# The third unit of the first attention's values goes between the pooling's products and the near products, and every later unit of both attentions goes one level sooner

## The chip, the cores and the metric

The kernel runs on one core of a Trainium2 chip. The metric is the device time of one execution in microseconds (us), lower is better.

## What is computed

A chain of blocks over a sequence of 512 tokens of width 1024, batch 1, all in float32: two hybrid layers (banded attention and chunkwise retention side by side), a SwiGLU feed-forward, a token mixer, a second feed-forward and a last norm. The change lies in the token mixer. Its input is projected by one weight matrix and split over four mixers, each 256 channels wide:

```python
p = (u @ w_in).astype(jnp.float32)
p_pool, p_hg, p_rw, p_gla = jnp.split(p, [G, 5 * G, 5 * G + RWKV_COLS], axis=-1)
y_pool = causal_multiscale_pool(p_pool, pool_w, pool_b, pool_scale)
hq, hf, hi, hg = jnp.split(p_hg, 4, axis=-1)
o_h = chunked_gated_linear_attention(silu(hq) * QK_SCALE, 1.0 - f, hi, log_f)      # HGRN
y_hgrn = rms_norm_2(o_h, hgrn_norm) * jax.nn.sigmoid(hg)
...                                                                              # RWKV-7 from p_rw
gq, gk, gv, gg, ga = jnp.split(p_gla, [G, 2 * G, 3 * G, 4 * G], axis=-1)
log_a = jax.nn.log_sigmoid(ga @ gla_w2 + gla_b) / GLA_GATE_TAU
o_g = chunked_gated_linear_attention(gq * QK_SCALE, gk, gv, log_a)                 # GLA
...
y = jnp.concatenate([y_pool, y_hgrn, y_rwkv, y_gla], axis=-1) @ w_out
```

Both linear attentions, the first ("hgrn") and the second ("gla"), have the form S_t = diag(a_t) S_(t-1) + k_t v_t, o_t = q_t S_t, with 4 heads of 64 channels.

## The kernel before, in words

**Engines and order.** The program is written out by hand, one instruction list for each engine, and semaphores tie them. Nothing reorders it: each engine works through its list, and waits at an instruction until the named semaphores have come.

**Units.** All large weights are streamed as units of 128x1024 (512 KB). SyncE loads a unit into one of four `raw` slots, in the order of a table (`unit_order`, L165 to L167). ScalarE (ACT) makes its rounded high part `w_high`, VectorE (DVE) the rest `w_low` (`split_through`, one instruction each on L2033 and L1260; these two lines are helpers, and most activations and tensor operations of the kernel have them), TensorE (PE) multiplies in three passes (`three_passes`, L500, L501, L502), 24 matmuls of 512 columns. There are three `w_high` and `w_low` slots. `use()`, called on ACT and DVE once for each unit in the places where PE takes it, makes the split of the unit two behind. PE waits for "weights split" of its unit.

**A linear attention.** `linear_attention(name, fill)` exists on PE, ACT and DVE. It first calls `fill(0)`. Then PE waits for the running sums of the decays ("decay summed") and makes the near products (L852, 32 matmuls of 128 columns in two pairs of banks), which DVE masks (`sb_near`). Then come nine levels, n from 0 to 8. On PE:

```python
for n in range(len(ORDER)):
    if n + 1 < len(ORDER):
        fill(n + 1)
    ...
    scores(n)
if name == "gla":
    fill(len(ORDER))
values()
if name == "hgrn":
    fill(len(ORDER))
```

`scores(n)` waits for "factors" of its level: DVE takes differences of the decays (`sb_E<-sb_c_hgrn`), ACT their exponential (`sb_E<-sb_E`), DVE multiplies with keys and queries (`sb_E<-sb_E,sb_kq_hgrn`). The products of levels 0 to 5 are on L865, those of the next ones on L876 and L879, `values()` on L891. `fill` is what is put between the levels: other work of the mixers, above all units.

**What the fills hold.** In the first attention: 4 units of its own values (tiles `w_mix_tok`, group 0), then `others`, 5 units for the second attention (gate, two queries, two keys; between the gate's unit and the first query's the small gate products `sb_ga,sb_gla_w` on L482), then 2 of the 4 units of the second attention's values. In the second one: the other 2, and 8 units for RWKV (`rwkv_steps`), with key norms (L482, from the squares `sb_y_rwkv` that ACT makes of mixed keys) and gates between them. DVE lands each RWKV unit (`sb_shifted<-bank,sb_inv_rms`) and mixes it.

**Values.** A value group holds four PSUM banks from its first unit to its last. When the last is done, ACT lands the four banks (`sb_v_hgrn`, `sb_v_gla`, "v landed by S"), and only then may their next users have them.

**Beside them.** At the head of the first attention stand the pooling's products (`pool_outputs`, L482 `sb_window,sb_pool_w`), whose four banks ACT reads (`sb_y_pool`). The end of the first attention's norm, `finish_hgrn` (square, sum and reciprocal on DVE, root on ACT `sb_small`), stands in the second one's `fill(0)`.

Of the kernel before, what the change touches and what calls it, by code (L numbers as in the profile page):

```python
# [141 lines left out]
def unit_order(t):  # L142

    order = []
    for n in range(2):
        product = lambda g: [t["w_tok"][n, g, u] for u in range(4)]
        order += [t["w_rot"][n, f] for f in range(8)] + product(0) + product(1) + product(2)
        order += [t["w_qk"][n, f] for f in QK_ORDER] + [t["w_ag"][n, f] for f in range(4)]
        order += [t["w_out"][n, g, half, pair] for g, half, pair in OUT_STEPS]

    def feed_forward(which):
        units = [t["w_ffn_in"][which, f] for f in range(2 * FT)]
        return units + [t["w_ffn_out"][which, f][:, a:min(a + UNIT, D_FF)]
                        for f in range(KT) for a in range(0, D_FF, UNIT)]

    def mixer_tiles(*tiles):
        return [t["w_mix_f"][f] for f in tiles]

    def mixer_group(g):
        return [t["w_mix_tok"][g, u] for u in range(4)]  # L160

    order += feed_forward(0)
    order += mixer_tiles(0, 1)
    order += mixer_tiles(10, 12, 11, 13) + mixer_group(0)
    order += [t["w_mix_ga"]] + mixer_tiles(14, 16, 15, 17)  # L165
    values, projections = mixer_group(1), mixer_tiles(*range(2, 10))
    order += values[0:3] + [projections[0], values[3]] + projections[1:]  # L167
    order += [t["w_mix_out"][f] for f in range(KT)] + [t["w_mix_out_rwkv"][u] for u in range(2)]
    return order + feed_forward(1)

# [282 lines left out]
def tensor_engine(e, s, mem, units):  # L453
# [371 lines left out]
    def mixers():  # L825
        m, n = mem.mix, MIX_NORM
# [123 lines left out]
        values_h, others, values_g = token_major("v", "hgrn", 1, n), gla_steps(), token_major("v", "gla", 1, n)  # L950

        def fill_hgrn(n):
            if n == 0:
                next(values_h)
                next(values_h)
                pool_outputs()
            else:
                next(values_h if n < 3 else others if n < 8 else values_g)

        linear_attention("hgrn", fill_hgrn)  # L960
        turn_values("hgrn", 0)
# [36 lines left out]
        projections = rwkv_steps()  # L998

        def fill_gla(n):  # L1000
            if n < 2:
                next(values_g)
                next(projections)
            elif n < 6:
                next(projections)
                if n == 4:
                    key_norms()
                if n in (2, 4):
                    next(projections)
                if n == 5:  # L1010
                    p.mark("xg read", MIX_NORM)
            elif n == 6:
                low_rank_gates()
            elif n == 9:
                output_gate()
# [233 lines left out]
def vector_engine(e, s, mem, units):  # L1249
# [359 lines left out]
    def mixers():  # L1609
# [157 lines left out]

        def fill_hgrn(n):
            if n == 0:
                next(values_h)  # L1770
                next(values_h)
            else:
                next(values_h if n < 3 else others if n < 8 else values_g)

        finish_hgrn = linear_attention("hgrn", fill_hgrn, lambda n: None, lambda n: None)

# [54 lines left out]

        def fill_gla(n):
            if n < 6:
                if n < 2:
                    next(values_g)
                if n == 0:
                    finish_hgrn()
                next(projections)
                if n in (2, 4):
                    next(projections)  # L1840
                    if n == 4:
                        floor_norms()
                    next(projections)
            elif n == 8:
                operand_steps()
# [175 lines left out]
def scalar_engine(e, s, mem, units, t):  # L2021
# [273 lines left out]
    def mixers():  # L2295
# [121 lines left out]
        def fill_hgrn(n):  # L2417
            if n == 0:
                next(values_h)
                next(values_h)  # L2420
                a.wait_ge(*of("pool shift"))
                for f in range(2):
                    for r in (slice(0, 64), slice(64, 128)):
                        a.wait_ge(*of("pool out", f, r.start))
                        act(m.y_pool[r, f, :], bank("pool out", f, r.start)[r, :], "y pool", f, r.start,
                            scale=mem.col("pool_scale", f, r), bias=small[r, 168 + f:169 + f])
            else:
                next(values_h if n < 3 else others if n < 8 else values_g)

        finish_hgrn = linear_attention("hgrn", fill_hgrn)  # L2430
        land_mixed("hgrn")
# [45 lines left out]
        projections = rwkv_steps()  # L2477

        def fill_gla(n):
            if n < 2:  # L2480
                next(values_g)
                if n == 0:
                    finish_hgrn()
                next(projections)
            elif n < 6:
                if n == 5:
                    low_rank_tanh()
                    spread_norms()
                next(projections)
                if n == 3:  # L2490
                    square_keys()
                if n in (2, 4):
                    next(projections)
            elif n == 6:
                sigmoids()
            elif n == 7:
                raise_decays()
            elif n == 9:
                land_gate()
# [431 lines left out]
```

## Time and profile before

| what | us |
|---|---|
| three runs | 1681.21, 1682.84, 1686.25 |
| their median | 1682.84 |
| the profiled execution, its own time | 1683.53 |
| its span | 1681.4 |
| PE busy in the span | 1638.9 (97%) |
| DVE busy | 862.1 (51%) |
| ACT busy | 667.8 (40%) |
| mean granted clock of TensorE | 0.986 |

The own time is the device time of the same execution that the trace shows; 2.1 us of it lie outside the span. Busy time is by the trace's instruction records. The first attention stands at about 988 to 1073 us of the span, the second at 1074 to 1161.

### The profile page before, as it was taken

How to read it: one execution, taken by the hardware profiler on the slowest of the kernel's cores; microseconds unless marked ns; L12 is line 12 of the kernel's file. 1: busy time of each engine (PE TensorE's matmuls, PEld its weight loads, DVE VectorE, ACT ScalarE, POOL GpSimd, SP SyncE). 2: the span in 40 equal slices, each digit the busy share in tenths (PEclk: the TensorE clock that was granted, in tenths of full speed). 3: DMA queues.
4: the chain of work that ended last, by engine and by line, in shares of the span. 5: the costliest groups of instructions: out<-in, count | busy, mean ns of one | idle time of the engine just before them, and what ended most of it. 6: DMA issues, size and time to landing. Idle time of an engine off the chain costs nothing.

```text
span 1681.4 us, 23771 instructions
## 1 busy us (share of the span) xinstructions
PE 1638.9 (97%) x9520; PEld 1328.4 (79%) x9520; DVE 862.1 (51%) x1170; ACT 667.8 (40%) x1018; POOL 127.2 (8%) x127
## 2 busy tenths in 40 slices
PE   9999999999999999999999999997999999999997
PEld 6877778877777888888888878785877888888886
DVE  6733445552444565444433478668557554444333
ACT  6145565314656433333323355346433433333221
POOL 0001001000100110000000310000410200000000
PEclk9999999999999999999999999998899999999998
DMA  5412212341221323322333322220012233222331
GB/s 181 154 63 76 88 51 88 113 126 63 71 81 51 101 76 112 100 91 98 91 96 102 135 81 65 63 63 1 14 36 82 88 101 100 94 94 84 102 103 50
DMA packets 40749, 144.13 MB, mean 86 GB/s; under 512 B 4816, under 2 KB 4832, under 8 KB 40256
## 3 DMA queue, kind: packets, MB, share of 16 engines
q1 hardware_dynamic: 37296, 131.61, 24.6%
q0 software_dynamic: 2192, 8.87, 1.6%
q10 hardware_dynamic: 1152, 2.14, 0.4%
q8 instruction: 75, 1.23, 0.3%
q14 instruction: 34, 0.28, 0.1%
HBM read 140.50 MB, written 2.10 MB: 85 GB/s over the span
## 4 chain that ended last, share of the span: by engine, by line
PE 88%; DVE 7%; ACT 3%; issue 1%; DMA 0%; DVEq 0%; SPq 0%; ACTq 0%
PE bank L500 26%; PE bank L502 25%; PE bank L501 25%; PE bank L482 2%; PE bank L1044 2%; PE bank L488 2%; PE bank L865 1%; PE bank L667 1%; PE bank L731 1%; PE bank L710 1%; DVE sb_w_low L1260 1%; ACT sb_w_high L2033 1%; PE bank L589 0%; DMA sb_x<-xT 0%; DVE sb_near L1674 0%
## 5 line engine op out<-in xcount | busy, mean ns | idle before, releaser
L1260 DVE TENSOR_TENSOR sb_w_low<-sb_raw,sb_w_high 128x1024 fp32r<-128x1024 f32 (+1 forms) x253 | 312.1, 1234 | 365.5 <-ACT sb_w_high L2033 359.0
L500 PE MATMUL bank<-sb_xg_high,sb_w_high 128*128 128x512 f32 x1176 | 465.4, 396 | 1.4 <-DVE sb_w_low L1260 1.4
L502 PE MATMUL bank<-sb_xg_high,sb_w_low 128*128 128x512 f32 x1176 | 458.7, 390 | 0.0
L501 PE MATMUL bank<-sb_xg_low,sb_w_high 128*128 128x512 f32 x1176 | 458.6, 390 | 0.0
L2033 ACT ACTIVATE sb_w_high<-sb_raw 128x1024 fp32r<-128x1024 f32 (+1 forms) x253 | 263.2, 1040 | 347.4 <-PE bank L502 323.2
L500 PEld LDWEIGHTS bank<-sb_xg_high,sb_w_high 128*128 128x128 f32 x1176 | 221.1, 188 | 63.3 <-issue 15.8
L502 PEld LDWEIGHTS bank<-sb_xg_high,sb_w_low 128*128 128x128 f32 x1176 | 221.2, 188 | 46.8
L501 PEld LDWEIGHTS bank<-sb_xg_low,sb_w_high 128*128 128x128 f32 x1176 | 221.3, 188 | 44.6 <-issue 0.2
L502 PE MATMUL bank<-sb_h_high,sb_w_low 128*128 128x512 f32 x352 | 136.9, 389 | 0.0
L500 PE MATMUL bank<-sb_h_high,sb_w_high 128*128 128x512 f32 x352 | 136.9, 389 | 0.0
L501 PE MATMUL bank<-sb_h_low,sb_w_high 128*128 128x512 f32 x352 | 136.9, 389 | 0.0
L500 PE MATMUL bank<-sb_w_high,sb_xg_high 128*128 128x512 f32 x256 | 103.0, 402 | 0.0
L501 PE MATMUL bank<-sb_w_low,sb_xg_high 128*128 128x512 f32 x256 | 100.1, 391 | 0.0
L502 PE MATMUL bank<-sb_w_high,sb_xg_low 128*128 128x512 f32 x256 | 99.9, 390 | 0.0
L2647 POOL TENSOR_TENSOR sb_square_sum<-sb_square_sum,sb_square 128x512 f32<-128x512 f32 x20 | 26.1, 1306 | 748.5 <-ACT sb_square L2033 748.5
L500 PEld LDWEIGHTS bank<-sb_h_high,sb_w_high 128*128 128x128 f32 x352 | 66.1, 188 | 13.8
L501 PEld LDWEIGHTS bank<-sb_h_low,sb_w_high 128*128 128x128 f32 x352 | 66.1, 188 | 13.7
L502 PEld LDWEIGHTS bank<-sb_h_high,sb_w_low 128*128 128x128 f32 x352 | 66.1, 188 | 13.6
L2033 ACT ACTIVATE sb_h_high<-sb_up 128x512 fp32r<-128x512 f32 x44 | 27.8, 632 | 115.6 <-DVE sb_up L1260 115.6
L1260 DVE TENSOR_TENSOR sb_up<-bank,sb_inv_rms 128x512 f32<-128x512 f32 x44 | 30.4, 691 | 78.0 <-PE bank L502 77.1
L2033 ACT ACTIVATE sb_gate<-sb_gate 128x512 f32<-128x512 f32 x44 | 27.8, 632 | 92.3 <-DVE sb_gate L1260 92.3
L500 PEld LDWEIGHTS bank<-sb_w_high,sb_xg_high 128*128 128x128 f32 x256 | 48.3, 189 | 17.1 <-issue 7.1
(344 smaller groups left out, 1965.9 us busy)
## 6 DMA issues: line engine op xcount, KB each, us to landing
sb_raw<-w_ffn_in SPq DMA_DIRECT2D x88, 512.0 KB, 3.5
sb_raw<-w_ffn_out SPq DMA_DIRECT2D x32, 512.0 KB, 3.5
sb_raw<-w_tok SPq DMA_DIRECT2D x24, 512.0 KB, 3.6
sb_raw<-w_mix_f SPq DMA_DIRECT2D x18, 512.0 KB, 3.5
sb_raw<-w_rot SPq DMA_DIRECT2D x16, 512.0 KB, 3.6
sb_raw<-w_qk SPq DMA_DIRECT2D x16, 512.0 KB, 3.4
sb_raw<-w_out SPq DMA_DIRECT2D x16, 512.0 KB, 3.4
sb_raw<-w_ffn_out SPq DMA_DIRECT2D x16, 384.0 KB, 3.1
```

The costliest lines, as they stand in the source:

```text
L482: made = e.matmul(out, lhsT, rhs, start=n == 0, stop=n == len(pairs) - 1)
L488: made = e.transpose(banks[i][:, blk(n)], in_, mem.ident)
L500: e.matmul(out, w[0], v[0], start=first, stop=False)
L501: e.matmul(out, w[0], v[1], start=False, stop=False)
L502: return e.matmul(out, w[1], v[0], start=False, stop=last)
L667: made = e.matmul(out[k], m.feat["rk"][r, f, blk(j)], m.feat["rq"][r, f, j * P:], start=part == 0, stop=part == 1)
L710: e.matmul(out[k], m.qT[r, j, blk(q)], m.kT[r, j, 0:keys], start=True, stop=True).then_inc(*p.up("scores", n, 2 * j + k, q))
L731: made = e.matmul(out[64 * k:64 * k + 64, blk(q)], m.tok["av"][:, key, h * ATT_DIM:(h + 1) * ATT_DIM], m.probT[:, 2 * (q % 2) + k, blk(key ...
L1044: made = e.matmul(out(banks[i], t, c), left(t, c), right(t, c), start=True, stop=True)
L1260: e.tensor_tensor(out, a, b, op).then_inc(*v.up(*signal))
L2033: e.activation(out, in_, func, bias=bias, scale=scale, accum_out=accum).then_inc(*a.up(*signal))
L2647: e.tensor_tensor(out, a, b, op).then_inc(*g.up(*signal))
```

## The change

The kernel text changes in the table of units and in the fills of the three engines.

- `fill_hgrn(0)` takes three value units instead of two. On PE the third stands behind `pool_outputs`, ahead of the near products. On ACT it stands behind the landing of the pooling's outputs.
- `fill_hgrn(n)`: the fourth value unit at n = 1 (before: the third at 1, the fourth at 2), the five `others` at n = 2 to 6 (before 3 to 7), three units of the second attention's values at n = 7, 8, 9 (before two, at 8 and 9).
- `fill_gla(0)` takes the last value unit of the second attention and the first of RWKV, `fill_gla(1)` only the second of RWKV.
- The table: the four value units of the second attention come together, then RWKV's. SyncE so loads the fourth ahead of RWKV's first.

No instruction is added or taken away.

```diff
@@ unit_order @@
-    values, projections = mixer_group(1), mixer_tiles(*range(2, 10))
-    order += values[0:3] + [projections[0], values[3]] + projections[1:]
+    order += mixer_group(1) + mixer_tiles(*range(2, 10))
@@ TensorE, fill_hgrn @@
                 next(values_h)
                 next(values_h)
                 pool_outputs()
+                next(values_h)
             else:
-                next(values_h if n < 3 else others if n < 8 else values_g)
+                next(values_h if n < 2 else others if n < 7 else values_g)
@@ TensorE, fill_gla @@
-            if n < 2:
+            if n == 0:
                 next(values_g)
-                next(projections)
-            elif n < 6:
+            if n < 6:
                 next(projections)
@@ VectorE, fill_hgrn @@
             if n == 0:
-                next(values_h)
-                next(values_h)
+                for _ in range(3):
+                    next(values_h)
             else:
-                next(values_h if n < 3 else others if n < 8 else values_g)
+                next(values_h if n < 2 else others if n < 7 else values_g)
@@ VectorE, fill_gla @@
             if n < 6:
-                if n < 2:
+                if n == 0:
                     next(values_g)
-                if n == 0:
                     finish_hgrn()
                 next(projections)
@@ ScalarE, fill_hgrn @@
                         act(m.y_pool[r, f, :], bank("pool out", f, r.start)[r, :], "y pool", f, r.start,
                             scale=mem.col("pool_scale", f, r), bias=small[r, 168 + f:169 + f])
+                next(values_h)
             else:
-                next(values_h if n < 3 else others if n < 8 else values_g)
+                next(values_h if n < 2 else others if n < 7 else values_g)
@@ ScalarE, fill_gla @@
-            if n < 2:
+            if n == 0:
                 next(values_g)
-                if n == 0:
-                    finish_hgrn()
-                next(projections)
-            elif n < 6:
+                finish_hgrn()
+            if n < 6:
                 if n == 5:
```

In the order of instructions, this is TensorE between the pooling's products and the near products, before and then changed (bank numbers are PSUM banks; in brackets the semaphores that a row waits for):

```order
L482 MATMUL bank4<-sb_window_1_145,sb_pool_w_1_124 64x512 [waits pooled,hgrn_q_landed]
L482 MATMUL bank5<-sb_window_1_145,sb_pool_w_1_124 64x512 [waits hgrn_k_landed]
L852 MATMUL bank2<-sb_kq_hgrn_1_130 128x128 [waits y_pool,decay_summed]
L852 MATMUL bank3<-sb_kq_hgrn_1_130 128x128
```
```order
L481 MATMUL bank5<-sb_window_1_145,sb_pool_w_1_124 64x512 [waits hgrn_k_landed]
L499 MATMUL bank6<-sb_w_high_1_51,sb_xg_high_1_66 128x512 [waits weights_split]
L500 MATMUL bank6<-sb_w_low_1_52,sb_xg_high_1_66 128x512
L501 MATMUL bank6<-sb_w_high_1_51,sb_xg_low_1_67 128x512
L852 MATMUL bank2<-sb_kq_hgrn_1_130 128x128 [waits y_pool,decay_summed]
```

The third value unit (bank 6, 24 rows of which three stand here) now waits for its split ahead of the near products; its place behind them is taken by the fourth. VectorE at the same place, before and then changed (`sb_c_hgrn` the decays, `sb_E` the factors):

```order
L1280 SCALAR_TENSOR_TENSOR sb_c_hgrn_131<-sb_mixer_120,sb_c_hgrn_131 128x512 x2
L1260 TENSOR_TENSOR sb_E_136<-sb_c_hgrn_131 128x16x32 x2
L1260 TENSOR_TENSOR sb_w_low_52<-sb_raw_50,sb_w_high_51 128x1024 x2
L1260 TENSOR_TENSOR sb_E_136<-sb_E_136,sb_kq_hgrn_130 128x1024
L1260 TENSOR_TENSOR sb_near_138<-bank,sb_shared_54 128x512 x4
L1260 TENSOR_TENSOR sb_E_137<-sb_c_hgrn_131 128x32x16 x2
```
```order
L1279 SCALAR_TENSOR_TENSOR sb_c_hgrn_131<-sb_mixer_120,sb_c_hgrn_131 128x512 x2
L1259 TENSOR_TENSOR sb_E_136<-sb_c_hgrn_131 128x16x32 x2
L1259 TENSOR_TENSOR sb_w_low_52<-sb_raw_50,sb_w_high_51 128x1024 x3
L1259 TENSOR_TENSOR sb_E_136<-sb_E_136,sb_kq_hgrn_130 128x1024
L1259 TENSOR_TENSOR sb_near_138<-bank,sb_shared_54 128x512 x4
L1259 TENSOR_TENSOR sb_E_137<-sb_c_hgrn_131 128x32x16 x2
```

A third split joins the two; the first of them is the third value unit's in both. ScalarE from the end of the first attention into the second (`sb_small` the root of the norm), before and then changed:

```order
L2033 ACTIVATE sb_w_high_51<-sb_raw_50 128x1024
L2033 ACT_TABLE_LOAD
L2033 ACTIVATE sb_small_60<-sb_small_60 128x4
L2033 ACTIVATE sb_w_high_51<-sb_raw_50 128x1024
L2033 ACTIVATE sb_mixed_147<-sb_shifted_148,sb_small_60 128x512
L2033 ACT_TABLE_LOAD
L2033 ACTIVATE sb_E_137<-sb_E_137 128x1024
L2033 ACTIVATE sb_w_high_51<-sb_raw_50 128x1024
L2033 ACTIVATE sb_v_gla_135<-bank,sb_inv_rms_t_59 128x512 x4
```
```order
L2031 ACTIVATE sb_w_high_51<-sb_raw_50 128x1024
L2031 ACTIVATE sb_v_gla_135<-bank,sb_inv_rms_t_59 128x512 x4
L2031 ACT_TABLE_LOAD
L2031 ACTIVATE sb_small_60<-sb_small_60 128x4
L2031 ACTIVATE sb_w_high_51<-sb_raw_50 128x1024
L2031 ACTIVATE sb_mixed_147<-sb_shifted_148,sb_small_60 128x512
L2031 ACT_TABLE_LOAD
L2031 ACTIVATE sb_E_137<-sb_E_137 128x1024
```

The landing of the second attention's values moved from behind the first mixing of RWKV to a place ahead of the norm's root.

## Rows read from the trace of the kernel before

**Rows 1.** Page, busy time of each engine.
```profile
PE 1638.9 (97%) x9520; PEld 1328.4 (79%) x9520; DVE 862.1 (51%) x1170; ACT 667.8 (40%) x1018; POOL 127.2 (8%) x127
```
**Rows 2.** Waits of PE: releaser, us in total, times, longest us.
```profile
PE bank L876 <- DVE sb_E L1260: 7.2, 1, 7.2
```
**Rows 3.** Timeline, PE, head of first attention: start, us, operation, [idle before <-releaser].
```profile
988.81 1.93 PE L482 MATMUL bank<-sb_window,sb_pool_w 64*64 64x512 f32 x8
...
992.37 1.16 PE L852 MATMUL bank<-sb_kq_hgrn 64*128 64x128 f32 x16 [1.63 <-ACT sb_y_pool L2033]
...
994.10 1.99 PE L852 MATMUL bank<-sb_kq_hgrn 64*128 64x128 f32 x16 [0.57 <-ACT sb_y_pool L2033]
...
996.01 0.79 PE L500 MATMUL bank<-sb_w_high,sb_xg_high 128*128 128x512 f32 x1
...
1004.38 0.50 PE L500 MATMUL bank<-sb_w_high,sb_xg_high 128*128 128x512 f32 x1
...
1010.05 2.00 PE L865 MATMUL bank<-sb_E 64*128 64x64 f32 x32
```
**Rows 4.** Timeline, DVE and ACT at the same place.
```profile
991.99 1.42 DVE L1260 TENSOR_TENSOR sb_E<-sb_c_hgrn 128x512 f32<-128x512 f32 x2
993.51 2.55 DVE L1260 TENSOR_TENSOR sb_w_low<-sb_raw,sb_w_high 128x1024 fp32r<-128x1024 f32 x2
994.03 1.28 ACT L2033 ACT_TABLE_LOAD   x1
...
995.33 1.06 ACT L2033 ACTIVATE sb_E<-sb_E 128x1024 f32<-128x1024 f32 x1
...
997.74 3.08 DVE L1260 TENSOR_TENSOR sb_near<-bank,sb_shared 128x512 f32<-128x512 f32 x4
...
1008.69 1.06 ACT L2033 ACTIVATE sb_w_high<-sb_raw 128x1024 fp32r<-128x1024 f32 x1
...
1010.16 2.85 ACT L2033 ACTIVATE sb_v_hgrn<-bank,sb_inv_rms_t 128x512 f32<-128x512 f32 x4 [0.41 <-PE bank L502]
```
**Rows 5.** Windows: stretch, us, PE, PEld, DVE, ACT, POOL busy, PEclk, DMA share, GB/s.
```profile
994.24:997.65 3.41, 3.41 (x20) 2.89 (x21) 2.95 (x3) 2.13 (x2) 0.00 (x0) 0.50 0.52 156
...
1021.54:1024.96 3.42, 3.42 (x9) 2.77 (x9) 3.07 (x5) 0.78 (x2) 0.00 (x0) 0.50 0.00 0
```
**Rows 6.** Timeline, PE, gate products and first query unit of the second attention.
```profile
1019.58 1.98 PE L482 MATMUL bank<-sb_ga,sb_gla_w 16*128 16x512 f32 x4
...
1021.49 0.78 PE L500 MATMUL bank<-sb_xg_high,sb_w_high 128*128 128x512 f32 x1
```
**Rows 7.** Timeline, head of the second attention: PE, ACT, DVE.
```profile
1074.40 0.48 PE L500 MATMUL bank<-sb_w_high,sb_xg_high 128*128 128x512 f32 x1
...
1078.31 1.28 ACT L2033 ACT_TABLE_LOAD   x1
...
1079.93 0.39 PE L500 MATMUL bank<-sb_xg_high,sb_w_high 128*128 128x512 f32 x1
...
1082.14 0.21 ACT L2033 ACTIVATE sb_small<-sb_small 128x4 f32<-128x4 f32 x1 [2.55 <-DVE sb_small L1276]
...
1082.38 0.18 DVE L1272 RECIPROCAL sb_small<-sb_small 128x4 f32<-128x4 f32 x1 [0.27 <-ACT sb_small L2033]
```
**Rows 8.** Timeline, DVE, ACT and PE on the way to the second attention's long wait.
```profile
1100.43 1.23 DVE L1260 TENSOR_TENSOR sb_w_low<-sb_raw,sb_w_high 128x1024 fp32r<-128x1024 f32 x1 [2.72 <-ACT sb_w_high L2033]
...
1123.73 1.48 ACT L2033 ACTIVATE sb_y_rwkv<-sb_mixed,sb_cols 128x512 f32<-128x512 f32 x2
...
1127.69 1.84 PE L482 MATMUL bank<-sb_mixer,sb_y_rwkv 128*128 128x2 f32 x16
...
1135.17 0.69 DVE L1260 TENSOR_TENSOR sb_shifted<-bank,sb_inv_rms 128x512 f32<-128x512 f32 x1 [2.35 <-PE bank L502]
...
1142.77 0.69 DVE L1260 TENSOR_TENSOR sb_shifted<-bank,sb_inv_rms 128x512 f32<-128x512 f32 x1 [0.70 <-PE bank L502]
...
1159.52 2.08 PE L876 MATMUL bank<-sb_E 64*128 64x128 f32 x16 [7.19 <-DVE sb_E L1260]
```

## The prediction

> **What bounds the kernel now.** I read four views in this order: the page, the waits of PE, the timeline of the two linear attentions on PE, DVE and ACT, and the windows of granted clock. The page says that PE is busy for 97% of the span [rows 1], so a reordering that leaves every instruction in place can only win PE's idle time and its slow stretches, or add to them. The view of PE's waits names one long one, 7.2 us for a factor of the second attention [rows 2]; the timeline puts its end at 1159.52 [rows 8]. The place that the change aims at is small: after the pooling's products, which end at 990.74, PE waits 1.63 us, then 0.57 us, for ACT's reads of the pooling's banks [rows 3]. Behind this idle time the clock is granted at 0.50 (1.2 GHz) from 994.24 to 997.65, against 1.00 (2.4 GHz) elsewhere [rows 5]; matmuls run there at half speed, so it costs half of 3.41, 1.7 us. All these sums are made against the profiled execution's 1683.53 us, 0.7 us above the median of the three runs, 1682.84. About 0.3%, 5 us, is what a measurement of this kernel can tell from no change.
>
> **1. The head of the first attention.** The third value unit is now ahead of the near products, and waits for its split. DVE makes that split as the first of two from 993.51 to 996.06 [rows 4], behind the running sums and the differences at 991.99, which stand ahead of it in both orders. Nothing upstream is earlier than before, so the split is ready at 993.51 + 1.28 = 994.8. PE is idle from 990.74 to 994.8, 4.06 us, in place of 1.63 + 0.57. Then it does the unit: 5.53 us by the neighbouring units of rows 7 (1074.40 to 1079.93), and if the slow stretch ends where it did, 2.85 us of it lie at half speed, which adds 1.43: about 1001.7. Near products: 32 in two pairs, each pair about 1.16 us as the first does [rows 3], to 1002.9 and 1004.0. The fourth unit: to 1009.6. Meanwhile DVE, which masks the near products in four steps (3.08 us), starts them at 1002.9 instead of 997.74, and comes to 1006.0, then the next differences (1.42) to 1007.5; ACT follows with an exponential and a split, 1.06 each [rows 4], to 1009.7, and only then lands the values, four steps in 2.85. The first level's products on PE used two banks that the near products had left; in the new order they take two of the values' banks, and wait for two landings, 1.43 us: 1011.2. They take 2.0 us as the next level's do [rows 3]: 1013.2. Before, the same work (four value units, near products, first level) was done at 1010.05 [rows 3]. **Cost: +3.2 us.** The bounds: if the landing comes right behind the fourth unit and the near products are hidden as before, 1009.6 + 1.4 + 2.0 gives 1013.0; if the low clock lasts as long after 994.8 as it did before after 994.24, 0.3 us more. The third split that DVE now makes in the pair costs 1.23 us of DVE at a place where it afterwards waits for PE (near products at 1002.9), so nothing; the table load and first exponential on ACT slip by one split, 1.06, under the same cover. SyncE's loads: two units of 512 KB change places, both still up to four slots ahead of their use; nothing, and if that cover were gone, ACT's split would wait for `sb_raw`.
>
> **2. One unit more ahead of the second attention.** Twelve units instead of eleven stand there, 5.6 us [rows 7]. **+5.6** on everything from its head: RWKV's first unit starts at 1079.93 + 3.2 + 5.6 = 1088.7. PE gets this unit back inside the second attention, but that stretch ends on something else (4).
>
> **3. The root of the first attention's norm.** ACT's list now has the landing of the second attention's values, 2.85 us [rows 4], ahead of the table load (1.28) and the root (0.21) [rows 7]. The landing waits for the last value unit, 1088.7; so 1088.9 + 2.85 + 1.28 + 0.21, and the gaps between them give the reciprocal on DVE at about 1093.35, against 1082.38 [rows 7]: +10.95, of which 8.8 are steps 1 and 2. **+2.15.** Queued behind the reciprocal on DVE are two products, a weight split and the landing of RWKV's first unit; behind the root on ACT a split and the first mixing. All of it is late with it.
> The Trainium skill ("ScalarE: Activation LUTs", What ACT_TABLE_LOAD costs) has a drain of about 1.38 us beside a load of about 1.28. The row shows the load at 1.28, and the next activation starts 0.02 us behind it [rows 4]. By the page the table load that now stands in the path would cost 1.4 us more (an estimate from that page), by the row nothing; I go by the row.
>
> **4. The second attention.** From the reciprocal (1082.38) to the last factors, released at 1159.5 [rows 8], DVE is nearly without a pause; this chain of 77 us, and not PE, sets when the attention ends, since PE waits 7.19 us for it. The change takes out of it: one split, 1.23 us and its gap, 1.33; the wait of 2.72 us for ACT's split, which stood behind the values' landing [rows 8] (landed earlier now); the wait of 2.35 us for RWKV's seventh unit, since PE now has a unit less in front; and of the wait of 0.70 for the eighth a part. How much of it hangs on the key norms: ACT's key squares end at 1125.2 and PE's norms start at 1127.69 [rows 8], 2.5 us later. The squares follow DVE, late by 10.95 - 1.33 - 2.72 = 6.9, so they end at 1132.1; PE would be there at 1127.69 + 3.2 = 1130.9 or sooner, waits, and is late by 4.4 from there. DVE, late by 6.9 - 2.35 = 4.55, is then released by PE again at 4.45: 0.1 of the 0.70. **-6.5.** Bounds: -7.1 (all of 0.70) and -5.8 (the 0.70 and 0.6 of the 2.35 stay, if PE is late by 5.1).
>
> **Sum:** 3.2 + 5.6 + 2.15 - 6.5 = **+4.45 us**: 1683.53 becomes 1688.0; against the median 1682.84, **1687.3**. The bounds of steps 1 and 4 give +3.7 to +5.5, 1686.5 to 1688.3. Behind the long wait nothing is changed. That is 0.26%, just inside what counts as the same.
>
> **The rivals.**
> A, the forecast, 0.48: of its bounds a good quarter lies above +5.05.
> B, *the clock fall behind the small gate products does not come back*, 0.18. Those products end and the clock is at 0.50 from 1021.54 for 3.42 us [rows 5, 6], with PE never idle: it costs 1.7. The rows at that place read the same in the new order, but come 3.2 us later and from another history. The sum is then 4.45 - 1.7 = +2.75, 1685.6. The Trainium skill ("TensorE: Matmul & The Clock Gate", Part 1: The HAM clock gate) ties falls of the clock to an idle PE and its release to activity; by it there would be no fall here, and the trace shows one with PE at work, so I leave it in.
> C, *a fall more, slower than before*, 0.17. Step 1 makes a wait of 1.6 us for the landed values ahead of the first level's products, and 4.06 us ahead of the third unit. Before, 2.2 us of waits were enough for a stretch of 3.41 us at 0.50. If the new wait of 1.6 brings one more such stretch, or the first is doubled by the longer wait, the price is again 1.7: +6.15, 1689.0 (+0.37%). It decides as soon as one window more at 0.50 lies between 990 and 1020. Against it: other waits of 0.5 to 2 us on PE have no low clock behind them, as the mean of 0.986 says.
> D, *the change does what it looks like*, 0.04: the third unit fills PE's wait. That takes a split ready at 990.74. Then 1.63 + 0.57 and the slow stretch's 1.7 go, -3.9, and with steps 2 to 4 (+1.25) the sum is -2.65, 1680.2; with the second attention's wait cut as well, up to its 7.2, it would be faster. DVE's row at 993.51 excludes it: sums and differences stand ahead of the split.
> E, *nothing comes out*, 0.10: the change does not do what it says for the end, since the second attention's chain gives the time back. It would need the chain to start from something other than the reciprocal, such as the decays' sums. Then steps 1 to 3 fall into PE's 7.19 us, and the time stays at 1682.8. Against it: DVE has no pause over 2.72 us from reciprocal to last factors.
> F, *the drain at the table load*, 0.03: +1.4, 1688.7.
>
> **How the numbers follow.** The prediction is A's 1687.3. Range: A, B, C and F together hold 0.86 and span 1685.6 to 1689.0; with C's and A's bounds, 1 us each way, and the spread of three runs, it is 1683.3 to 1690.6. Outside are D and most of E. Slower by over 0.3% (above 1687.9): C, F and 0.15 of A, 0.35. Faster by over 0.3% (below 1677.8): the far part of D and what I may have overlooked, 0.05. The same: 0.60.
>
> **What would show it.** Right: PE idle for 4 us ahead of the third unit, released by `sb_w_low`, the pooling's waits gone; a wait of 1.5 to 2 us for `sb_v_hgrn` ahead of the first level's products; the reciprocal 11 us later; a wait of 1 to 2 us at the key norms, for `sb_y_rwkv`; the long wait for the last factors still about 7 us, since PE, late by 4.4 from the key norms on, and the chain of DVE, late by 4.45, are late alike. Wrong: if the third unit starts before 993.5, step 1 falls; if the reciprocal is less than 9 us late, step 3 does; if DVE keeps a wait of 2 us for RWKV's seventh unit, step 4's sum is too large; a window more or less at 0.50 is C or B.

## The result, and the profile after

The changed kernel takes 1695.52 us (median of 4 runs, 1694.12 to 1699.29) against 1682.03 of the kernel before (4 runs, 1680.95 to 1686.25): the ratio is 1.0076, interval 1.006 to 1.0092. In a second measurement it was 1693.54 (6 runs, 1688.48 to 1697.62) against 1683.88 (29 runs), ratio 1.0058, interval 1.0037 to 1.0079. It is slower by 0.6 to 0.8%; 1687.3 was forecast, and the range ended at 1690.6. The profiled execution of the changed kernel took 1694.68 us with a span of 1691.8, 11.15 us more than the profiled one before.

The page of the changed kernel, busy time; then its view of the waits of PE (releaser, us in total, times, longest us).

```profile
PE 1644.1 (97%) x9520; PEld 1332.2 (79%) x9520; DVE 862.5 (51%) x1170; ACT 667.8 (39%) x1018; POOL 126.9 (8%) x127
```
```profile
PE bank L499 <- DVE sb_w_low L1259: 6.0, 4, 4.1
PE bank L875 <- DVE sb_E L1259: 6.0, 1, 6.0
...
PE bank L864 <- ACT sb_v_hgrn L2031: 1.9, 1, 1.9
...
PE bank L481 <- ACT sb_y_rwkv L2031: 1.8, 1, 1.8
```

The wait for the pooling's reads is gone [rows 3]; three waits that were not there have come: 4.1 us for a weight split, 1.9 for the first attention's values, 1.8 for the key squares. The instructions are the same in number, and yet PE is busy for 5.2 us more: some of them ran slower. The timeline of the changed kernel at the head, DVE, ACT and PE, answers to [rows 3, 4]:

```profile
989.12 1.93 PE L481 MATMUL bank<-sb_window,sb_pool_w 64*64 64x512 f32 x8
...
993.92 3.88 DVE L1259 TENSOR_TENSOR sb_w_low<-sb_raw,sb_w_high 128x1024 fp32r<-128x1024 f32 x3
...
995.20 0.80 PE L499 MATMUL bank<-sb_w_high,sb_xg_high 128*128 128x512 f32 x1 [4.14 <-DVE sb_w_low L1259]
...
1003.64 2.06 PE L851 MATMUL bank<-sb_kq_hgrn 64*128 64x128 f32 x32
...
1004.83 3.08 DVE L1259 TENSOR_TENSOR sb_near<-bank,sb_shared 128x512 f32<-128x512 f32 x4 [5.62 <-PE bank L851]
...
1011.73 2.84 ACT L2031 ACTIVATE sb_v_hgrn<-bank,sb_inv_rms_t 128x512 f32<-128x512 f32 x4
...
1013.28 2.36 PE L864 MATMUL bank<-sb_E 64*128 64x64 f32 x32 [1.92 <-ACT sb_v_hgrn L2031]
```

The third unit starts as its split is ready, and takes from 995.20 until the near products start at 1003.64, 8.4 us, where its neighbours take 5.5. The windows of granted clock say why (stretch, its us, PE, PEld, DVE, ACT, POOL busy, PEclk, DMA share, GB/s), and show what became of the other places, [rows 5] of before:

```profile
996.20:1000.80 4.60, 4.60 (x12) 3.61 (x11) 2.72 (x3) 1.74 (x2) 0.00 (x0) 0.50 0.83 275
1015.00:1017.80 2.80, 2.80 (x11) 2.27 (x11) 2.06 (x3) 0.67 (x1) 0.00 (x0) 0.50 0.37 139
1022.50:1032.00 9.50, 9.50 (x61) 6.91 (x60) 6.26 (x8) 3.15 (x4) 0.00 (x0) 1.00 0.14 52
1138.00:1140.80 2.80, 2.80 (x8) 2.13 (x8) 1.92 (x2) 0.69 (x1) 0.00 (x0) 0.50 0.12 24
...
1187.00:1194.00 7.00, 7.00 (x61) 6.87 (x61) 1.98 (x5) 2.09 (x4) 1.45 (x2) 0.50 0.00 0
```

The first low stretch is twice as long (994.29 to 1001.12, and PE works in 5.9 us of it), one follows the wait for the values, the one behind the gate products is not there, one follows the wait at the key norms, and in the inverse there is one more. At the second attention, ACT, DVE and PE, the answers to [rows 7, 8]:

```profile
1093.89 1.28 ACT L2031 ACT_TABLE_LOAD   x1
...
1095.18 0.20 ACT L2031 ACTIVATE sb_small<-sb_small 128x4 f32<-128x4 f32 x1
...
1095.42 0.18 DVE L1271 RECIPROCAL sb_small<-sb_small 128x4 f32<-128x4 f32 x1 [2.49 <-ACT sb_small L2031]
...
1143.64 0.69 DVE L1259 TENSOR_TENSOR sb_shifted<-bank,sb_inv_rms 128x512 f32<-128x512 f32 x1 [1.74 <-PE bank L501]
...
1151.24 0.69 DVE L1259 TENSOR_TENSOR sb_shifted<-bank,sb_inv_rms 128x512 f32<-128x512 f32 x1 [0.70 <-PE bank L501]
```
```profile
1134.47 1.92 PE L481 MATMUL bank<-sb_mixer,sb_y_rwkv 128*128 128x2 f32 x16 [1.79 <-ACT sb_y_rwkv L2031]
...
1167.98 2.08 PE L875 MATMUL bank<-sb_E 64*128 64x128 f32 x16 [5.97 <-DVE sb_E L1259]
```

Three steps lead to the end. The head: at the first unit behind the first attention's levels (1078.85, before 1068.03) the kernel is 10.8 us late, of which one unit is 5.6. The reciprocal of the norm: 13.0 late. The last factors of the second attention: 8.5 late, so the second attention gave back 4.6. Behind them, 1.9 more.

Two theories for the experiments. **Theory 1**: the order of the work costs about what the sum said, and the rest is TensorE's clock, which falls to 1.2 GHz after the new waits; each fall costs 1.7 us where PE works in it. **Theory 2**: the order costs all of it, by a chain that the sum has wrong, and the clock only goes along.

### The profile page after: what moved, and what is told of

It reads as the page before. It is cut to its first block, busy times and chain, and to the rows that moved or that the text cites. A ratio compares the mean times of both kernels' runs of the same rounds, so it can differ in the third digit from the quotient of the medians.

```text
span 1691.8 us, 23771 instructions
## 1 busy us (share of the span) xinstructions
PE 1644.1 (97%) x9520; PEld 1332.2 (79%) x9520; DVE 862.5 (51%) x1170; ACT 667.8 (39%) x1018; POOL 126.9 (8%) x127
## 4 chain that ended last, share of the span: by engine, by line
PE 86%; DVE 9%; ACT 3%; issue 1%; DMA 0%; DVEq 0%; SPq 0%; ACTq 0%
PE bank L499 25%; PE bank L501 24%; PE bank L500 24%; PE bank L481 2%; PE bank L1043 2%; PE bank L487 2%; PE bank L666 1%; PE bank L730 1%; DVE sb_w_low L1259 1%; PE bank L709 1%; DVE sb_E L1259 1%; PE bank L864 1%; ACT sb_w_high L2031 1%; DVE sb_near L1673 1%; PE bank L588 0%
## 5 line engine op out<-in xcount | busy, mean ns | idle before, releaser
L499 PEld LDWEIGHTS bank<-sb_h_high,sb_w_high 128*128 128x128 f32 x352 | 66.1, 188 | 13.5
L1259 DVE TENSOR_TENSOR sb_up<-bank,sb_inv_rms 128x512 f32<-128x512 f32 x44 | 30.4, 692 | 77.9 <-PE bank L501 77.1
```

Source lines behind the costliest of these rows:

```text
L499: e.matmul(out, w[0], v[0], start=first, stop=False)
L1259: e.tensor_tensor(out, a, b, op).then_inc(*v.up(*signal))
```

## The experiments

**The same kernel again**, as the yardstick of the second measurement.

> The changed kernel once more, beside the others of this call. If its 1.0076 is a property of the kernel: 1.006 to 1.009 of before. If part of it was the chip of that measurement: 1.004 to 1.006.

1693.54, ratio 1.0058: in the second range of the expectation, with an interval (1.0037 to 1.0079) that reaches through both. Its profiled execution has the same four waits, and its low stretches lie differently: one of 3.4 us behind the first wait instead of one of 6.8, one of 6.8 at 1013 to 1020, and the one behind the gate products is back, at 1026.85. So the stretches are not a fixed property of the order: the same program shows others from one execution to the next.

**The third unit's split ahead of the running sums** (VectorE):

```diff
         tt(c2, c2, low, ALU.add, *STEP)
+        split_through(used[0] + SPLIT)
```

> The changed kernel, with VectorE's split of the third value unit moved ahead of the running sums. Theory 1 (PE's 4.14 us wait for that split at the head, and the two stretches of 1.2 GHz behind it, 994.0 to 1001.5, are the larger part of the loss there): the wait falls to under 0.5 us, the low stretch behind it goes, and the time falls by 4 to 8 us against the changed kernel, to about 1688 to 1691. Theory 2 (the head costs nothing in the end, because the wait for the landed values ahead of the first level's products and the rest of the chain behind it set the pace): the wait goes, but the level's wait grows by as much, and the time stays within 2 us of the changed kernel's 1695.5.

1690.43 (5 runs), ratio 1.0047 (1.0031 to 1.0062), 3 to 5 us less than the changed kernel. The split now ends as the pooling's products do, the unit follows them, and neither the wait nor the stretch at 994 is there. But the wait for the values has grown to 3.17, and a stretch at 1.2 GHz (1009.8 to 1013.2) still follows it. Timeline of early_split, DVE, PE and ACT:

```profile
990.51 1.23 DVE L1259 TENSOR_TENSOR sb_w_low<-sb_raw,sb_w_high 128x1024 fp32r<-128x1024 f32 x1
991.79 0.50 PE L499 MATMUL bank<-sb_w_high,sb_xg_high 128*128 128x512 f32 x1
...
997.46 2.06 PE L851 MATMUL bank<-sb_kq_hgrn 64*128 64x128 f32 x32
...
1008.35 2.41 PE L864 MATMUL bank<-sb_E 64*128 64x64 f32 x32 [3.17 <-ACT sb_v_hgrn L2032]
```

**Unread products in three waits.** PE does work that nobody reads while it would wait: 6 ahead of the third unit (into the bank that the near products take next), 3 ahead of the first level, 3 at the key norms.

```diff
                 pool_outputs()
+                i = take(("unread", turn[0]), None)
+                for _ in range(6):
+                    e.matmul(banks[i][:, :], mem.ones, mem.inv_rms, start=True, stop=True)
+                turn[0] -= 1
                 next(values_h)
```

(TensorE; the places of the other 3 and 3 are not shown.)

> The changed kernel with unread products of 512 columns (the form that the kernel already uses to keep PE busy) in three of PE's waits: 6 ahead of the third unit, 3 ahead of the first level's products, 3 ahead of the key norms. No wait is shortened for the other engines. Theory 1 (extra stretches at 1.2 GHz follow PE's idle time, 1.7 us each): the stretches at 994 to 1001.5, 1014.5 to 1018.5 and 1137.5 to 1141.5 go or shrink, and the time falls by 3 to 5 us against the changed kernel, to about 1691. Theory 2 (the schedule alone costs the time, the clock is an accompaniment): the same stretches at 1.2 GHz or others in their place, and the time within 1 us of the changed kernel's.

1687.98 (5 runs), ratio 1.0037 (1.0025 to 1.005): 5.6 to 7.5 us less than the two medians of the changed kernel, although nothing was made ready sooner and the unread products even ran over the waits. In the timeline and windows of busy_waits the third unit starts at 997.0, 1.8 us later than in the changed kernel, and the near products still come 1.2 us sooner, since PE has 2.4 GHz there.

```profile
991.61 5.42 PE L962 MATMUL bank<-sb_inv_rms,sb_ones 128*128 128x512 f32 x12 [0.57 <-ACT sb_y_pool L2041]
1002.44 2.06 PE L851 MATMUL bank<-sb_kq_hgrn 64*128 64x128 f32 x32
```
```profile
994.40:1001.20 6.80, 6.80 (x26) 4.60 (x25) 4.20 (x4) 3.26 (x3) 0.00 (x0) 1.00 0.68 213
...
1014.80:1018.00 3.20, 3.20 (x15) 2.62 (x15) 2.99 (x5) 1.71 (x2) 0.00 (x0) 1.00 0.01 4
...
1134.00:1141.00 7.00, 7.00 (x45) 5.77 (x44) 5.13 (x7) 1.82 (x3) 1.22 (x1) 1.00 0.20 59
```

One such product takes 0.9 us (5.42 / 6). Theory 2 falls here: the order is that of the change, with work added, and half of the loss or more is gone.

**The same, apart and nearly without overrun**: stay_head has 4 and 2 unread products at the head (the third unit starts 0.3 us later than in the changed kernel) and none at the key norms, stay_keys 2 at the key norms alone.

> The changed kernel with unread products only in the two waits at the head (4 of 0.9 us ahead of the third unit, 2 ahead of the first level's products), sized so that they do not overrun the waits. Theory 1 (idle time brings the stretches at 1.2 GHz): those at 994 to 1001.5 and 1014.5 to 1018.5 are gone, the last factors of the second attention come 3 to 5 us sooner than in the changed kernel, and the time is 3 to 5 us less. Theory 2: stretches and time as in the changed kernel.

> The changed kernel with 2 unread products in the wait at the key norms alone. Theory 1: the stretch at 1137.5 to 1141.5 is gone, the wait for the last factors ends 1.7 us sooner (VectorE's wait of 1.74 for RWKV's seventh unit goes), the time 1.5 to 2.5 us less than the changed kernel; the stretches at the head stay. Theory 2: the stretch moves to the next small products, nothing is won.

stay_head: 1688.18 (12 runs), ratio 1.0029 (1.0018 to 1.004), 5.4 less than the changed kernel's second median. No stretch at 1.2 GHz is left at the head, and the last factors come 4.3 us sooner, counted from the pooling's products. Windows of stay_head:

```profile
996.00:1003.00 7.00, 7.00 (x55) 5.74 (x54) 3.72 (x5) 1.95 (x2) 0.00 (x0) 1.00 0.69 225
...
1014.00:1019.00 5.00, 5.00 (x35) 4.03 (x33) 4.62 (x6) 2.13 (x2) 0.00 (x0) 1.00 0.00 0
```

stay_keys: 1692.9 (6 runs), ratio 1.0052 (1.0033 to 1.007). The interval covers the changed kernel's, so the gain of 1.5 to 2.5 us that was expected is not shown in the time. In the trace it is. The stretch at the key norms is gone, VectorE has no wait left for RWKV's seventh unit, and from the reciprocal to the last factors it is 70.9 us, where the changed kernel has 72.6 and the kernel before 77.1. DVE and PE of stay_keys:

```profile
1097.63 0.18 DVE L1273 RECIPROCAL sb_small<-sb_small 128x4 f32<-128x4 f32 x1 [2.49 <-ACT sb_small L2033]
...
1144.23 0.69 DVE L1261 TENSOR_TENSOR sb_shifted<-bank,sb_inv_rms 128x512 f32<-128x512 f32 x1
...
1168.50 1.86 PE L875 MATMUL bank<-sb_E 64*128 64x128 f32 x14 [7.09 <-DVE sb_E L1261]
```

**The tail alone**: the head as before the change (two units ahead of the near products), the twelfth unit as a second one in the last fill. TensorE, without the line that is taken out of `fill_hgrn(0)`; ScalarE and VectorE have the same:

```diff
-                next(values_h if n < 2 else others if n < 7 else values_g)
+                next(values_h if n < 3 else others if n < 8 else values_g)
+                if n == 9:
+                    next(values_g)
```

> The head of the first attention as before the change (two units, near products, the third and fourth unit at levels 1 and 2), the tail as changed: three units of the second attention's values in the first attention (the third one as a second unit in the last fill), one in the second. Theory 1 (head and tail both cost; of the profile's +11.2 us the head's part at the start of the second attention is 4.9, the rest 5 to 6 is the tail's): 1686 to 1688, 4 to 6 us above before. Theory 2 (the second attention gives the unit back, as the sum had it, +1.25 and no clock loss): 1683.3. Theory 3 (almost all the loss is the tail's): above 1691.

1686.72 (9 runs, 1681.41 to 1689.08), ratio 1.0016 (1.0004 to 1.0028). The median, 3.8 us above before's 1682.94, lies in the first theory's range; the interval of the ratio, 0.7 to 4.7 us, reaches from under the second theory's 1.25 into the first's. Either way the tail is the smaller part. Its profiled execution (1683.1, 3.6 us below its median) has the last factors 1.7 us later than before, counted from the pooling's products (1162.01 - 989.64 against 1159.52 - 988.81), with the same time at 1.2 GHz up to the key norms. Forecast was 1.25. Its head shows one thing more: the pooling's waits of 1.55 and 0.57 us are those of before, and no fall of the clock follows them. Window of tail_alone:

```profile
994.00:1001.00 7.00, 6.43 (x44) 5.28 (x41) 6.02 (x8) 3.06 (x3) 0.00 (x0) 1.00 0.46 150
```

**The root ahead of the landing** (ScalarE; `finish_hgrn()` moves into the last value step, behind the weight's split):

```diff
                 if u == KT // 2 - 1:
+                    if name == "gla":
+                        finish_hgrn()
                     a.wait_ge(*of("v", name))
```

> The changed kernel with the root of the first attention's norm ahead of the landing of the second attention's values on ScalarE. Theory 1 (that order is 2.15 us or more of the loss, and with it the wait of 1.79 us at the key norms and the stretch at 1.2 GHz behind it go): 1691.5 to 1693.5, 2 to 4 us less than the changed kernel. Theory 2 (the second attention is held by PE's side, so the earlier reciprocal only lengthens DVE's waits): within 1 us of the changed kernel's 1695.5.

1688.3 (5 runs), ratio 1.0035 (1.0022 to 1.0048). That is more than expected, and the trace says that not all of it is the root's. ACT and DVE of root_first:

```profile
1096.01 0.21 ACT L2031 ACTIVATE sb_small<-sb_small 128x4 f32<-128x4 f32 x1 [2.55 <-DVE sb_small L1275]
1096.25 0.18 DVE L1271 RECIPROCAL sb_small<-sb_small 128x4 f32<-128x4 f32 x1 [0.27 <-ACT sb_small L2031]
1096.31 2.85 ACT L2031 ACTIVATE sb_v_gla<-bank,sb_inv_rms_t 128x512 f32<-128x512 f32 x4
```

DVE's wait at the reciprocal fell from 2.49 to 0.27, 2.2 us: the term of the sum to the tenth. Not all of it arrives: a few operations later DVE waits 1.40 us for a split that ACT now makes behind the landing (1100.34). PE's wait at the key norms is still there, 1.25 instead of 1.79, and here no fall of the clock follows it. The last factors (178.8 us behind the pooling's products) are as late as the changed kernel's, since this execution lost 1.3 us more at 1.2 GHz ahead of them; what it gained came in the inverse behind them, where it lost 3.4 us at 1.2 GHz instead of 8.5.

**Both repairs, and the banks.** all_three lets the first level's products go to the near products' banks as before the change (`turn[0] += 4` ahead of them).

> Both repairs on the changed kernel: the third unit's split ahead of the running sums, and the norm's root ahead of the landing of the second attention's values. Theory 1 (head and root are separate losses, since they lie in different chains): the gains of 5 and 7 us add, 1683 to 1685. Theory 2 (both worked by way of the same thing, the stretches at 1.2 GHz late in the second attention and in the inverse, which move about with any shift): no more than the better of the two, 1687 to 1689.

> early_root, and the first level's products go to the banks that the near products left instead of the values' banks. Theory 1 (the wait for the landed values, 3.2 us once the split is early, is idle time that counts): the wait is gone, 2 to 4 us less than early_root. Theory 2 (the level's factors or the next levels' chain set the pace there): within 1 us of early_root.

early_root: 1688.55 (12 runs), ratio 1.0026 (1.0009 to 1.0042). The two gains do not add in the time. all_three: 1682.78 (12 runs), ratio 0.9991 (0.9979 to 1.0004), level with before, and 5.8 less than early_root, where 2 to 4 were expected. The wait for the landed values, 3.2 us in early_root, is gone; PE and ACT of all_three:

```profile
997.00 2.06 PE L851 MATMUL bank<-sb_kq_hgrn 64*128 64x128 f32 x32
...
1004.65 2.00 PE L864 MATMUL bank<-sb_E 64*128 64x64 f32 x32
...
1006.33 2.85 ACT L2034 ACTIVATE sb_v_hgrn<-bank,sb_inv_rms_t 128x512 f32<-128x512 f32 x4
```

**The clock in the kernel before.** late_stay_before puts 1, 7, 2 and 2 unread products into PE's waits of 1.65, 7.19, 2.0 and 2.6 us; gate_stay_before 2 behind the gate products.

> The kernel before the change, with unread products (1, 7, 2 and 2 of 0.9 us each) in four of PE's late waits: 1.65 and 7.19 us in the second attention, 2.0 and 2.6 in the inverse. Theory 1 (the stretches at 1.2 GHz at 1151 to 1165, 1178.5 to 1185.5 and 1192 to 1199 follow PE's idle time and cost what PE works in them at half speed): the work behind 1159.5 runs at 2.4 GHz, 4 to 8 us less than before, 1675 to 1679. Theory 2 (the low clock comes with the small products there, not with idleness): the same stretches, and the time within 1 us of before or above it by what the unread products overrun.

> The kernel before, with 2 unread products (1.8 us of PE) right behind the small gate products of 16 rows. Theory 1 (the fall to 1.2 GHz at 1021.5, where PE was not idle, comes from the small products ahead of it: 64x64 of the third level and 16x512 of the gates): it is not taken away by work put behind them, and the time is 1 to 2 us more than before. Theory 2 (the fall is left over from idle time at the head): no fall, and the time is before's.

late_stay_before: 1679.46 (12 runs), ratio 0.9979 (0.9968 to 0.999), faster than before by 2 to 5 us. Two stretches of its windows, then the same two of the kernel before:

```profile
1151.00:1159.50 8.50, 7.77 (x43) 4.00 (x40) 8.02 (x7) 6.01 (x8) 2.36 (x1) 1.00 0.01 2
1159.50:1165.00 5.50, 4.54 (x32) 2.85 (x34) 5.08 (x7) 4.29 (x8) 0.00 (x0) 1.00 0.00 0
```
```profile
1151.00:1159.50 8.50, 1.32 (x16) 1.14 (x14) 8.09 (x7) 6.08 (x8) 2.35 (x1) 0.51 0.00 0
1159.50:1165.00 5.50, 5.49 (x27) 4.27 (x28) 5.02 (x7) 3.60 (x7) 0.00 (x0) 0.51 0.01 3
```

The gain, 4.4 us, is at the low end of what was expected: from 1177.0 to 1187.3 this execution still had 1.2 GHz. gate_stay_before: 1687.25 (12 runs), ratio 1.0024 (1.0013 to 1.0034), 2 to 6 us slower, which is the 1.8 us of added work and some more. Its execution has no fall at the gate products, where before had one, and one of 6.8 us at the head, where before had 3.4. It does not tell its two theories apart.

**The best version.** all_stay is all_three with the late unread products and one at the key norms.

> all_three with unread products in the late waits (1, 7, 2, 2 as in late_stay_before) and 1 at the key norms. If the repaired order's gain and the late clock's gain add: 4 to 6 us below before, 1677 to 1679. If late_stay_before has taken all there is: its 1679.5 to 1680.5.

1677.3 (12 runs, 1673.08 to 1680.44), ratio 0.9964 (0.9953 to 0.9975): 4 to 8 us faster than before, and 16 less than the changed kernel's 1693.5. The gains of all_three and of late_stay_before about add. At the key norms a wait of 0.3 us was left, and a stretch of 3.4 us at 1.2 GHz followed the one unread product.

One table puts the traces together. For each profiled execution: the last factors of the second attention (the start of the products that waited for them) less the start of the pooling's products; the time lost at 1.2 GHz between the two, which is half of the time that PE worked in stretches at 1.2 GHz, up to 1145; both as differences to before (170.7 and 3.4); and their difference, the part of the order. The last column is an estimate: it counts every loss as if it reached the last factors in full.

| kernel | last factors | at 1.2 GHz | order |
|---|---|---|---|
| after | +8.2 | +3.0 | +5.2 |
| after_again | +9.9 | +5.1 | +4.8 |
| stay_head | +3.8 | -1.7 | +5.5 |
| stay_keys | +8.5 | +3.4 | +5.1 |
| root_first | +8.1 | +4.3 | +3.8 |
| early_split | +2.4 | 0 | +2.4 |
| tail_alone | +1.7 | 0 | +1.7 |
| early_root | +4.6 | +3.3 | +1.3 |
| all_three | -0.1 | +1.7 | -1.8 |
| gate_stay_before | +1.6 | -0.2 | +1.7 |
| late_stay_before | +0.2 | 0 | +0.2 |

The last two rows test the estimate: late_stay_before has the order of before up to there and reads 0.2, gate_stay_before has 1.8 us of added work and reads 1.7. The unrepaired order reads 4.8 to 5.5 in four executions. The split takes 2.4 to 2.8 us from it, the root 1.1 to 1.4, the banks 3.1 more. busy_waits (+4.9, -3.4, +8.3) and all_stay (-1.5, 0, -1.5) are not in the table, since their unread products are work of their own.

The granted clock of every run, and not only of the profiled ones, agrees. The changed kernel's six runs of the second measurement lie between a span of 1686.7 us at a mean clock of 0.987 and 1695.5 at 0.981, in strict order of the clock, 1.5 us for each 0.001. Of the 29 runs of the kernel before beside them, the seven at 0.987 have a mean span of 1682.6 and the five at 0.986 one of 1684.3; the changed kernel has one run each there, 1686.7 and 1688.2. So at the same clock it is about 4 us slower, which is the order. The other 6 of its 10 us go with the clock, 0.984 on the mean against 0.988. early_root's twelve runs fall apart in the same way: five at 0.984 with a mean span of 1689.7, three at 0.988 with 1680.6, which is level with before (1681.0 at 0.988). The clock hides there what the two repairs gained.

## Why the prediction was wrong

The forecast was A, +4.45; the profile's difference is +11.15, the medians' 9.7 and 13.5. The order cost about what was forecast. The step that failed is the price of the clock: step 1 let the slow stretch end where it did before, with a bound of 0.3 us, and put nothing behind the new waits. The span's 10.4 us more are 0.3 by which the pooling's products already started later, 5.2 of order, 3.0 lost at 1.2 GHz up to the last factors, and 1.9 behind them. Without the last two the profiled execution would have taken 1689.8, inside the range.

- **Step 1, the third unit waits for its split** (forecast: idle 4.06 us): measured 4.14, released by `sb_w_low`. The wait for two landed values was forecast at 1.6 and was 1.92. The order's part of head and tail together is 4.8 and 5.2 in the two executions against 4.45 (4.7, when the 0.3 is left out that the forecast won in the slow stretch: 1.43 for 1.7), within the bounds of 3.7 to 5.5. What failed is the sentence "if the slow stretch ends where it did", and its bound of 0.3 us: the low clock lasted to 1001.12, where PE lost 3.0 us and not 1.43, and it came again at 1014.77 for 1.7. In stay_head and busy_waits, where unread products fill the waits, neither is there, and in all four executions that have both waits both are.
- **Step 2, a unit more**: right, the unit is 5.6 of the 10.8.
- **Step 3, the root**: +2.15, measured 2.2 by root_first. The reciprocal came 13.04 late instead of 10.95. The difference, 2.1, is about what step 1 left out: 1.5 of clock (1.5 more in the third unit, one stretch more, B's less), 0.3 by the later start of the pooling's products, and 0.4 in the two waits of step 1. Between table load and root the row shows 0.01 us, and between landing and table load 0.08, so there is no drain in the path.
- **Step 4, the second attention gives back 6.5**: 4.6. The split and the 2.72 us wait went as forecast. PE's wait at the key norms came (1.79, forecast 1 to 2), and behind it a stretch at 1.2 GHz made PE late enough that DVE kept 1.74 of its 2.35 us and all 0.70 for RWKV's last units. The forecast had that wait and did not put a fall of the clock behind it. In the trace of stay_keys this is all but the whole error: without the fall the second attention gives back 6.3 us, 77.14 less 70.87.
- **"Behind the long wait nothing is changed"**: the instructions were not, the time was, by 1.9 us in the two executions of the changed kernel (span less last factors, 523.8 and 523.9 against 521.9), with one stretch of 3.4 us at 1.2 GHz more in the inverse of the first one. In the other executions this part took from 518.0 to 526.5.
- **The rivals.** C had the right mechanism, a chance of 0.17 and +6.15. It asked for one fall more, behind the wait for the values *or* in a first stretch doubled. Both came, which by its own price is +7.85, 1690.7; then one at the key norms and one in the inverse, less the one of B at the gate products, which indeed did not come back in the first execution. D, E and F are out. The argument against C, that other waits of 0.5 to 2 us have no low clock behind them, does not hold in the trace that it was read from. In the kernel before, PE works again at 1149.87 behind 1.65 us and at 1176.32 behind 2.00, and each time the clock is at 0.50 within 2.3 us (from 1151.25 and from 1178.56); the mean of 0.986 contains these stretches. Behind 1.71 us, which end at 1280.27, there is none; so a wait of this length can bring a fall and need not. Timeline, then windows, of the kernel before:

```profile
1149.87 2.46 PE L865 MATMUL bank<-sb_E 64*128 64x64 f32 x32 [1.65 <-DVE sb_E L1260]
...
1176.32 0.69 PE L1035 MATMUL bank<-sb_kkE,sb_bI 64*64 64x64 f32 x32 [2.00 <-DVE sb_rE L1260]
```
```profile
1151.25:1152.30 1.05, 1.05 (x12) 0.89 (x10) 1.02 (x2) 0.99 (x3) 0.00 (x0) 0.50 0.00 0
1178.60:1185.30 6.70, 6.70 (x36) 6.64 (x32) 2.62 (x6) 2.39 (x4) 1.45 (x2) 0.50 0.00 0
```

- **The chances and the range.** Slower had 0.35. The order alone stood 0.6 us below the bound of 0.3%, and every new wait could only add. The range's ends, 1683.3 and 1690.6, do not follow from the terms that the prediction names for them.

What stays open is why the same wait is followed by a longer stretch, a shorter one or none, and which falls come without idle time ahead of them. That the runs of one kernel spread over 11 us (before: 1677.78 to 1689.3) goes with the clock: of the 29 spans, the seven at 0.988 have a mean of 1681.0, the five at 0.986 of 1684.3, the four at 0.990 of 1678.7. Which stretches make the difference is seen in the profiled executions alone.

## What to carry to other kernels

Price a new wait of PE at its length and at the half speed that may follow it: here a wait of about 4 us cost another 1.7 to 3.0, and waits of 1.1 to 1.9 us, ahead of the first level's products and at the key norms, cost another 1.7 to 3.4 in all cases but one. Before moving a unit up, move what it waits for as well: the split on DVE, the root on ACT and the choice of banks together turned about 5 us of order into -1.8. Where the wait must stay, products that nobody reads, sized to end with it, can give back the clock; they were worth 5 us in the changed kernel and 4 in the one before. And compare two orders by spans at the same granted clock, or with the clock's part taken out: the profiled executions here lie up to 3.6 us from the medians of their kernels, on either side.

## What the hardware showed that was not expected

- The low clock can stay for 6.8 us behind a wait of 4.1 (granted 0.50 from 994.29 to 1001.12 in after, PE busy throughout from 995.20). Behind the same wait it was 3.4 in after_again. Behind the kernel before's two waits of 1.6 and 0.6 at that place it was 3.4 in before and 6.8 in gate_stay_before, and there was none in tail_alone and late_stay_before.
- The same program shows other stretches from execution to execution: 3.4 or 6.8 us of them behind the first wait, 3.4 or 6.8 behind the wait for the values, one or none behind the gate products.
- Falls with PE at work ahead of them exist, at the gate products: in the kernel before at 1021.54, and in seven more of the fourteen profiled executions, among them all_three and all_stay, where all waits at the head are gone. In all_three PE had no wait from 990.8 on, and then had 1.2 GHz for 6.8 us. In after, with the same instructions as after_again, there was no such fall, nor in busy_waits and stay_head. So filling or removing the head's waits does not by itself take it away. The Trainium skill ("TensorE: Matmul & The Clock Gate", Part 1: The HAM clock gate) ties the throttled state to an idle PE; the falls that stay_head took away agree with it, the ones of before and all_three, with PE at work ahead of them, do not. Windows of all_three:

```profile
990.80:1015.60 24.80, 24.74 (x175) 19.53 (x172) 21.82 (x25) 13.67 (x16) 0.00 (x0) 1.00 0.32 94
1015.70:1022.40 6.70, 6.70 (x15) 4.47 (x14) 4.22 (x6) 3.66 (x5) 0.00 (x0) 0.50 0.10 40
```

- ACT's table load showed no time beside its 1.28 us: it starts 0.08 behind the landing, and the root 0.01 behind it.
